# One decoder layer with an expert layer: 88 of 256 tokens by gathered rows and 168 dense, the second gate and the first key scores moved into the query phase, a sixth block buffer

## The reference, cut to what matters

```python
q = (hc @ wq).reshape(T, 8, 2, 128)
s1 = einsum('thd,hnd->thn', q[:, :, 0], sub_keys[:, 0])   # 128 key scores, first half
s2 = einsum('thd,hnd->thn', q[:, :, 1], sub_keys[:, 1])
v1, i1 = top_k(s1, 16);  v2, i2 = top_k(s2, 16)
sc, ci = top_k(all 256 sums v1 + v2, 16)
e = i1[ci // 16] * 128 + i2[ci % 16]
act = gelu(einsum('td,thkd->thk', hc, exp_u[e]))
out = einsum('thk,thkd->td', softmax(sc) * act, exp_v[e])
x = x + gate2(c) * out;  then a final RMSNorm
```

## Time and profile before

| | |
|---|---|
| median of 3 runs (lowest, highest) | 861.15 us (858.42, 862.43) |
| the profiled execution: time / span from first to last instruction | 859.74 us / 857.9 us |
| granted TensorE clock | 0.997 of 2.4 GHz |
| PE busy / VectorE busy | 833.6 us / 548.3 us |
| bytes moved | 277.94 MB |

### The profile page before, as it was taken

The page is one execution under the profiler, slowest core; times in us unless marked ns, Lnnn a source line. Parts: engine busy times, 40 slices in busy tenths (PEclk is TensorE's granted clock), DMA queues, the critical chain, the costliest instruction groups (busy, mean ns, idle before and its releaser), DMA issues.

```text
span 857.9 us, 14450 instructions
## 1 busy us (share of the span) xinstructions
PE 833.6 (97%) x5758; PEld 806.1 (94%) x5758; DVE 548.3 (64%) x1113; ACT 172.7 (20%) x452; POOL 198.4 (23%) x201
## 2 busy tenths in 40 slices
PE   6999999999999999999999999999999999999996
PEld 4998879889999999999999999989999999999996
DVE  5859889755998998678788887743344445342002
ACT  5464585523111112111111111000000000000003
POOL 2000000000103333633343435433333233231000
PEclk9999999999999999999999999999999999999998
DMA  9998791702878998999999999999999999999771
GB/s 337 402 386 319 306 395 47 313 6 79 234 244 301 388 392 270 406 408 408 368 350 353 358 364 361 406 410 370 408 392 402 379 399 410 384 373 315 222 234 58
DMA packets 72644, 277.94 MB, mean 324 GB/s; under 512 B 8225, under 2 KB 10513, under 8 KB 71298
## 3 DMA queue, kind: packets, MB, share of 16 engines
q1 hardware_dynamic: 48626, 191.52, 59.1%
q0 software_dynamic: 23952, 85.50, 26.8%
HBM read 275.50 MB, written 1.49 MB: 323 GB/s over the span
## 4 chain that ended last, share of the span: by engine, by line
PE 90%; DVE 4%; DMA 3%; ACT 1%; issue 1%; another core or an unknown queue 1%; SPq 0%; ACTq 0%; DVEq 0%
PE banks L1218 35%; PE banks L1189 34%; PE banks L925 3%; PE banks L858 3%; PE banks L1201 2%; PE banks L878 2%; PE banks L921 2%; DMA raw<-in_v_b 1%; PE banks L863 1%; DMA raw<-in_u_t 1%; PE banks L994 1%; DVE sc_w L1328 1%; PE banks L834 1%; PE banks L1178 1%; PE banks L894 1%; PE banks L1083 1%
## 5 line engine op out<-in xcount | busy, mean ns | idle before, releaser
L1189 PE MATMUL banks<-hT,raw 128*128 128x176 f32 x2048 | 311.3, 313 | 1.8 <-DMA raw<-in_u_t 1.5
L1218 PE MATMUL banks<-act,raw 128*128 128x176 f32 x2048 | 308.8, 313 | 1.7 <-DMA raw<-in_v_b 1.7
L1218 PEld LDWEIGHTS banks<-act,raw 128*128 128x128 f32 x2048 | 305.6, 190 | 3.6 <-DMA raw<-in_v_b 3.5
L1189 PEld LDWEIGHTS banks<-hT,raw 128*128 128x128 f32 x2048 | 305.5, 190 | 2.5 <-DMA raw<-in_u_t 2.0
L1652 DVE SCALAR_TENSOR_TENSOR sum_pair<-rows,weight,sum_pair 128x1024 f32<-128x1024 f32 x63 | 80.9, 1285 | 103.9 <-DMA rows<-in_v_b,idx 103.0
L541 POOL DMA_INDIRECT rows<-in_v_b,idx x80 | 90.4, 1130 | 174.0 <-PE banks L1218 129.2
L541 POOL DMA_INDIRECT rows<-in_u_rows,idx x80 | 95.4, 1192 | 138.9 <-DVE dots L1630 120.8
L1630 DVE CUSTOM_DVE_ANT_0 rows<-rows,h_pair 128x1024 f32<-128x1024 f32 x64 | 77.2, 1222 | 8.9 <-DMA rows<-in_u_rows,idx 4.6
L790 ACT ACTIVATE turned<-banks,g_col 128x256 f32<-128x256 f32 x8 | 3.8, 473 | 307.5 <-PE banks L1218 307.5
L748 ACT ACTIVATE act<-banks 128x176 f32<-128x176 f32 (+21 forms) x123 | 34.1, 277 | 125.2 <-PE banks L1189 120.4
L505 POOL DMA_DIRECT2D h_lines<-h_stage x1 | 0.5, 527 | 209.5 <-ACT h_stage L773 209.5
(11 more groups left out here) (248 smaller groups left out, 862.8 us busy)
## 6 DMA issues: line engine op xcount, KB each, us to landing
raw<-in_u_t SPq DMA_DIRECT2D x128, 512.0 KB
raw<-in_v_b SPq DMA_DIRECT2D x128, 512.0 KB
wq<-in_wq SPq DMA_DIRECT2D x2, 4096.0 KB, 18.0
sh_w<-in_w_mod SPq DMA_DIRECT2D x8, 512.0 KB, 12.5
sc_w<-in_w_mod SPq DMA_DIRECT2D x8, 512.0 KB, 13.5
win<-in_w_in SPq DMA_DIRECT2D x8, 512.0 KB, 14.2
win<-in_w_in SPq DMA_DIRECT2D x1, 4096.0 KB, 20.9
sc_w<-in_w_mod SPq DMA_DIRECT2D x2, 2048.0 KB, 23.1
```

The lines of the kernel that those rows point to most:

```text
L1189: last = nc.tensor.matmul(dst, raw[n % RAW][:, c * P:(c + 1) * P], hT[:, c, 0:MANY], start=(c == 0), stop=(c == DC - 1))
L1218: return nc.tensor.matmul(chunk_place(c)[:, 0:MANY], raw[(BLOCKS + j) % RAW][:, c * P:(c + 1) * P], act[:, j, :], start=(j == 0 and c < 4) ...
```

## The change

- The gathered tokens are `KINDS = (64, 16, 8)`, so `FEW` = 88, `MANY` = 168; there are 88 row tiles for u and 88 for v, three row copies of the normed tokens (`h2_rows`), three tile sums and three folds. 21 gate groups are left.
- `RAW` = 6 block buffers; the sixth lies where small columns were held.
- The second gate runs in the query phase: SP loads its 8 chunks through the first five block buffers before the first u block, and VectorE multiplies them in groups 2 to 5. The broadcast row `crow2`, its copy in memory and the waits for it are gone.
- Key scores of four lists (two halves of the tokens) are computed after groups 2, 4, 6 and 7; six of the twenty steps of the first sort move into the query phase.
- `EARLY_SLOTS` 4 to 6, `EXP_AT` 49 to 50, `GATE_AT` 59 to 60.
- In the u phase the gathers from the 24th on also wait for a block count (`PACE_U` = 1 block each).

```diff
-RAW = 5
-PAIRED = 64
-SPREAD = 16
-FEW = PAIRED + SPREAD
+RAW = 6
+GATE_RAW = 5
+KINDS = (64, 16, 8)
+FEW = sum(KINDS)
-EARLY_SLOTS = 4
+EARLY_SLOTS = 6
-GATE_AT = 59
+GATE_AT = 60
+PACE_U = 1.0
+        QUAD_AFTER = (2, 4, 6, 7)
...
+            for c in range(DC):
+                if c >= GATE_RAW:
+                    sp.wait_ge(sc2_read, DC + c - GATE_RAW + 1)
+                sp.dma_start(raw[c % GATE_RAW][:, :], w_mod[4][:, c, :]).then_inc(shift_in[c], 16)
             for n in range(STREAM):
+                if n < RAW:
+                    sp.wait_ge(sc2_read, DC + (n + 1 + GATE_RAW if n + GATE_RAW < DC else n + 1 if n < GATE_RAW else DC))
                 if n >= RAW:
                     sp.wait_ge(block_used, n - RAW + 1)
                 sp.dma_start(raw[n % RAW][:, :], u_t[n] if n < BLOCKS else v_b[n - BLOCKS]
                              ).then_inc(raw_full[n % RAW], 16)
-                if n == BLOCKS + ROW_LOAD:
-                    sp.wait_ge(lines_moved, LINE_SAVED)
-                    sp.dma_start(crow2[:, :], c_lines.ap().broadcast_to([P, D])).then_inc(crow2_in, 16)
-                since = n - BLOCKS - G2_LOAD
-                if 0 <= since < 8 * DC and since % 8 == 0:
-                    c = since // 8
-                    sp.dma_start(g2_w[:, c, :], w_mod[4][:, c, :]).then_inc(shift_in[c], 16)
...
+                if EARLY + 4 < i < TILES:
+                    pool.wait_ge(block_used, TURN_AT + int((i - EARLY - 4) * PACE_U))
                 if i >= TILES + AHEAD:
                     pool.wait_ge(block_used, BLOCKS + int((k - AHEAD) * PACE))
...
+            def key_scores(f):
+                if f == 0:
+                    pe.wait_ge(loaded["keys"], 16)
+                    pe.wait_ge(proj_out, N_IN + 2)
+                else:
+                    pe.wait_ge(q_sum, 2 * f)
+                    pe.wait_ge(s_out, 2 * f)
+                for g in range(2 * f, 2 * f + 2):
+                    t = 1 - g % 2
+                    for l in range(4 * f, 4 * f + 4):
+                        last = nc.tensor.matmul(bank[s_bank(g)][:, l % 4 * P:(l % 4 + 1) * P],
+                                                qT[:, l, t * P:(t + 1) * P], keys[:, l, :], start=True, stop=True)
+                    last.then_inc(s_ready, 1)
...
                 query_wide(WQ + g, g)
+                if g in QUAD_AFTER:
+                    key_scores(QUAD_AFTER.index(g))
...
+                    for n in range(len(KINDS)):
+                        nc.tensor.matmul(chunk_place(c)[:, MANY + KIND_AT[n]:MANY + KIND_AT[n + 1]],
+                                         row_sums[n][:, c * P:(c + 1) * P], folds[n][:, :], start=False, stop=False,
+                                         skip_group_check=True)
...
+            GATE_CHUNKS = {2: (0, 1, 2), 3: (3,), 4: (4, 5), 5: (6, 7)}
             for g in range(LISTS // 2):
                 for e in range(2):
                     low_part(WQ + g, (e, e + 1), weights_low)
                 if g >= 3:
                     query_sum(g - 1)
+                for c in GATE_CHUNKS.get(g, ()):
+                    second_gate(c)
+                if g == 5:
+                    ve.wait_ge(sc2_read, 2 * DC)
+                    nc.vector.tensor_scalar(g2_col[:, :], g2_col[:, :], 1.0 / GATE_SCALE, None, ALU.mult
+                                            ).then_inc(acc_ready, 1)
+                sort_quads({6: 2, 7: 4}.get(g, 0))
             query_sum(LISTS // 2 - 1)
+            sort_quads(LISTS // 4 * 5 - quad_steps[0])
```

More of the change, by code:

```diff
@@ L35 @@
 STREAM = 2 * BLOCKS
-RAW = 5
-PAIRED = 64
-SPREAD = 16
-FEW = PAIRED + SPREAD
+RAW = 6
+GATE_RAW = 5
+KINDS = (64, 16, 8)
+FEW = sum(KINDS)
 MANY = SEQ - FEW
 FEW0 = P - FEW
-TILES = PAIRED + SPREAD
+TILES = FEW
+KIND_AT = [sum(KINDS[:n]) for n in range(len(KINDS) + 1)]
 GATHERS = 2 * TILES
-EARLY_SLOTS = 4
+EARLY_SLOTS = 6
 EARLY = 18
@@ L170, in hybrid_peer_layer, with small_table @@
         corr = at("corr", R[4] + 2048, [P, 2, 2, SEQ])
-        raw_word = [RAW0, RAW0 + D, R[4], R[4] + D, R[4] + 3 * D]
+        raw_word = [RAW0, RAW0 + D, R[4], R[4] + D, R[4] + 3 * D, G20]
         raw = [at(f"raw{n}", raw_word[n], [P, D]) for n in range(RAW)]
[L173 to L179, removed]
+        table_word = [R[4] + 2048]
+        def small_table(name, shape, dt=F32):
+            n = 1
+            for s in shape[1:]:
+                n *= s
+            t = at(name, table_word[0], shape, dt)
+            table_word[0] += n if dt != F16 else n // 2
+            assert table_word[0] <= R[4] + 3 * D
+            return t
+        idx = small_table("idx", [P, TILES], U32)
+        gate_few = small_table("gate_few", [P, TILES])
+        dots = small_table("dots", [P, TILES])
+        weight = small_table("weight", [P, TILES])
+        keys_h = small_table("keys_h", [P, 2, MANY], F16)
+        folds = [small_table(f"fold{n}", [P, count]) for n, count in enumerate(KINDS)]
         v = at("v", RAW0, [P, TT, D])
@@ L1168, in _ @@
                 query_wide(WQ + g, g)
-            pe.wait_ge(loaded["keys"], 16)
-            for g in range(TT * LISTS // 4):
-                t, four = 1 - g % 2, g // 2
-                if g in (0, 6):
-                    pe.wait_ge(q_sum, LISTS // 2 - 3 if g == 0 else LISTS // 2 - 2)
-                if g >= 4:
-                    pe.wait_ge(s_out, g - 3)
-                for e in range(4):
-                    l = 4 * four + e
-                    last = nc.tensor.matmul(bank[s_bank(g)][:, e * P:(e + 1) * P], qT[:, l, t * P:(t + 1) * P],
-                                            keys[:, l, :], start=True, stop=True)
-                last.then_inc(s_ready, 1)
+                if g in QUAD_AFTER:
+                    key_scores(QUAD_AFTER.index(g))
             def u_block(n):
@@ L1602, in query_sum, with second_gate, top16_step, top16 @@
                                         ALU.add).then_inc(q_sum, 1)
+            def second_gate(c):
+                ve.wait_ge(shift_in[c], 32)
+                w = raw[c % GATE_RAW]
+                nc.vector.tensor_tensor_reduce(out=w[:, :], in0=w[:, :], in1=crow[:, :], scale=1.0,
+                                               scalar=bcol[:, 4, c:c + 1], op0=ALU.mult, op1=ALU.add,
+                                               accum_out=g2_col[:, c:c + 1]).then_inc(sc2_read, 1)
+            def top16_step(vals, pos, src, lists, step):
+                k = step // 3 * 8
+                for l in lists:
+                    if step % 3 == 0:
+                        last = nc.vector.max(vals[:, l, k:k + 8], src(l))
+                    elif step % 3 == 1:
+                        last = nc.vector.max_index(pos[:, l, k:k + 8], vals[:, l, k:k + 8], src(l))
+                    else:
+                        last = nc.vector.match_replace(src(l), vals[:, l, k:k + 8], src(l), -3.0e38)
+                link(last)
+            def top16(vals, pos, src, n, between):
+                for step in range(5):
+                    top16_step(vals, pos, src, range(n), step)
+                    between()
+            GATE_CHUNKS = {2: (0, 1, 2), 3: (3,), 4: (4, 5), 5: (6, 7)}
+            quad_steps = [0]
+            def sort_quads(n):
+                for _ in range(n):
+                    f, step = quad_steps[0] // 5, quad_steps[0] % 5
+                    if step == 0:
+                        ve.wait_ge(s_out, 2 * f + 1)
+                    top16_step(top_v, top_iu, lambda l: score[:, 1, l, :], range(4 * f, 4 * f + 4), step)
+                    quad_steps[0] += 1
             for g in range(LISTS // 2):
```

165 lines of the change are left out of this document (59 added, 106 removed).

## The result

| | time, us | profiled execution | span | u stage begins | v stage begins | folds begin |
|---|---|---|---|---|---|---|
| before | 861.79 (858.42 to 863.12) | 859.74 | 857.9 | 203.43 | 535.48 | 835.04 |
| after | 847.85 (846.01 to 849.73) | 847.37 | 845.6 | 205.21 | 525.48 | 818.01 |

The forecast was 22.5, and 838 with a range of 831 to 846; the measured 847.85 is outside it.

A forecast was written before the change was run, and what follows sets the result against it. PE was taken as the bound, with transfers close behind. Terms of -27.2, -0.9, +1.8, +1.35, -0.7 and +3.2 summed to -22.5 us, from 859.74 to 837.3, stated as 838, range 831 to 846.

The forecast's parts named there:

- Dense columns, gate group: In u and v: 8 columns fewer in 4096 recorded matmuls, -27.2 us; one gate group fewer, -0.92 us.
- Key scores: End of the query phase: PE waits for group 7's query sum before the last key scores, +1.35 us.
- The second gate in the query phase, the sort, the gate phase: Query phase through gates: VectorE's added and moved work fits, 0.2 us in hand per three blocks; nothing lost.
- rival D: Gate phase: VectorE becomes the bound, a late tile stops gelu and then PE; 866 or more, chance 0.04.
- The row copies at the start of u: Start of u: three 512 KB copies, but the sixth buffer adds reserve; loss 1 us instead of 1.7, -0.7 (-1.7 to +2).
- The v stage: v: queued gathers take half the transfers, a block per 2.56 us against 2.28 wanted; 6.3 us lost, net +3.2.
- so 2.5 with a sixth buffer. It lasts 45 us: v: reserve of 2.5 blocks instead of 1.5 delays the shortage 45 us; then about 58 us at 2.56 a block.
- Folds: After v's main blocks: three folds instead of two per chunk, 16 more recorded matmuls, +1.8 us.
- A: v: no shortage, since the reserve is deeper or the last dots sooner done; 6 us less, 832, chance 0.22.
- B: v: shortage over all the tiles, gathers and stream together wanting 411 GB/s; 19 us lost, 850, chance 0.09.
- C: Late start: low parts wait for gate chunks, or row copies starve PE; 3 to 6 us more, 842, chance 0.07.

The follow-up runs named there:

- the pair of runs with late copies: Spread folds, paced v gathers, second and third row copy after the eighteenth gather: 836.9 us; the same with block 0 ahead of the last eight key scores: 835.97 us.
- the three other traces: Changed kernel with folds spread over the last four blocks (843.34 us), with v gathers paced from the start (839.38), and with both (835.68).
- fold_spread: Changed kernel with the 48 fold matmuls put chunk by chunk between the last four v blocks' products: 843.34 us, ratio 0.9809 to before.
- the two with other row copies: Changed kernel without the third row copy: 844.23 us; changed kernel with the three copies made from 128 distinct rows of the u table: 842.42 us.
- the spaced run: Changed kernel with v gathers paced from the start, 2 instead of 10 ahead and one per 1.38 blocks instead of 1.45: 839.38 us, ratio 0.977.

## Why the prediction was wrong

**Dense columns, gate group.** Right: 142.7 ns against 142.8, 27.2 us.

**Key scores.** Right in kind, 0.4 us small. PE idled 1.48 us in front of L879, until VectorE's last sum. It was worth nothing to remove it, as the pair of runs with late copies shows; that the transfers bound the first third of u was not in the forecast.

**The second gate in the query phase, the sort, the gate phase.** Right: nothing was lost. In the gate phase three blocks took 6.89 us and the gates 0.92, as forecast, and rival D's wait did not come.

**The row copies at the start of u.** Wrong, and outside the bounds of -1.7 to +2. I took a loss of 1 us, because "the sixth buffer is one block more of reserve". The loss in the first 55 blocks was 5.9, and 3.8 to 4.4 in the three other traces, against 1.7 before: +4.2, or +2.1 to +2.7. The rate of 224 to 257 GB/s in the earlier trace rows was read as the price of 1 MB of copies in any form; the run with other rows moved 329 to 407 GB/s with 1.5 MB and lost nothing, so it was the price of these copies from this source. Why the source is slow stays open. A part of the error was hidden by luck: the 1.5 us that before lost between 350 and 380 us were gone in after, and no term of the forecast had that.

**The v stage.** The mechanism was right: tiles weighed every 2.55 us, as VectorE's timeline of after shows below and as the earlier trace rows showed, blocks at the same 2.55, the queue gone after 101 us where 103 was forecast. The first gather left as v began and not 1 us before it.

```profile
538.49 0.75 DVE L1692 TENSOR_SCALAR row_sums<-rows,weight 128x1024 f32<-128x1024 f32 x1 [0.42 <-DMA rows<-in_v_b,idx]
541.05 1.29 DVE L1695 SCALAR_TENSOR_TENSOR row_sums<-rows,weight,row_sums 128x1024 f32<-128x1024 f32 x1 [1.81 <-DMA rows<-in_v_b,idx]
```

The step that failed is "so 2.5 with a sixth buffer. It lasts 45 us". The shortage began 16 us into v (21 at most in the other kernels with six buffers and 168 dense tokens), not 45: the forecast counted a full reserve from v's first block, but the last u gathers already filled the transfers from about 512 us, 13 us before v, and it was being spent from there. By the forecast's own rate what was left for v was 16 x 0.048 = 0.8 blocks where it had 2.5. From there 85 us at 2.55 a block cost 85 x (1 - 2.28/2.55) = 9.0 us, where 58 us and 6.3 had been forecast. The working had slips of its own as well: the two parts of the 1.5 blocks add to 0.028 x 38 + 1 = 2.1, and 2.5 blocks at 0.048 last 52 us and not 45. The step was wrong by its size only, and by 3.1 us; the kernels that keep the burst of gathers, fold_spread and the two with other row copies, lost 9.7 to 10.2 us in v, so this size is no accident of one trace.

**Folds.** Wrong by 3.3 us. I priced a fold by its time at full clock, and the sum holds only there. In one piece the 48 folds ran at a granted 0.79 and the block behind at 0.55. The price itself was right: where the clock held until their end they took 5.26 us, 1.8 more than the 3.48 of the 32 before. What had been put at nothing was the clock, 3.3 us in the changed kernel and about 1.7 where it fell late. No row of before showed it, as 32 folds did not do it.

**The rivals.** A (no shortage in v) was excluded by the trace; so was B, since the shortage of after ended 101 us into v, and the spaced run excludes it again. C's second half, that "the row copies starve PE", came true together with the forecast's own shortage; it had been written as something instead of it. The three misses all have one sign and add to 3.4 + 3.1 + 3.3 = 9.8 of the 10.2 us by which the spans fell short. That is for the profiled execution; by the three other u stages the first miss is 1.3 to 1.9. (From the median of three, 861.15, the sum gives 838.65, not 838.)

**Best version.** Spread folds and spaced gathers are enough: 0.9718 against 0.9842. The two with late copies are at 0.9698 and 0.9683, whose intervals overlap with its own.

## What to carry to other kernels

Where a second queue is served half of the transfers while it holds anything, issue its transfers one by one as they are needed: a burst "to be ahead" is paid by the stream beside it, and the bytes alone say nothing. A reserve of buffers is spent from when the transfers last had idle time, so look for that place before the stage, not at its first block. Before a cause is read from a difference of 1 or 2 us in one stage, look at the same stage in runs that do not touch it. Work with few columns is priced with the clock at which its whole run will go, and costs less between long matmuls than in one piece.

## What was not expected of the hardware

- Copies of 64, 16 and 8 rows of a scratch tensor in DRAM, read 2, 8 and 16 times, went with 185 to 211 GB/s over all queues while they ran; with as many bytes from distinct rows of an input it was 329 to 407, at shares of the transfer engines of 0.77 and 1.02 against 0.89 and 1.02. Repetition alone is not shown to be the reason: one row read 128 times on SP's queue left 408 GB/s.
- The granted clock fell to 1.2 GHz after 48 folds of 64, 16 and 8 columns had begun in one piece, in six kernels of six: in the changed kernel within them (6.51 us in all, the block behind 4.44), in three others only as they ended (5.26 us, the block behind 3.95 to 4.06). It stayed at 1.00 with 32 in one piece (3.48 us), and with 48 in eight groups of six between longer ones. Whether the number, the length or the 8 columns matter was not tried.
- A full transfer system kept PE fed at 408 GB/s with spaced gathers, and starved it at 409 GB/s with queued ones.
